# Layers' attentions: VectorE takes the remainder of a split head right behind the step's maximum

## The reference, cut to what matters

```python
h = rms_norm(x, g_mix[layer]);  proj = h @ w_in[layer]
# A: 8 heads of 64; each query sees the 128 keys that an indexer's scores pick (top_k)
p = softmax(where(valid, q_a @ k_a.T * scale, -inf));  out_a = p @ v_a
# B, differential: 4 heads with two query/key pairs of 64 and one value of 128 each
p = softmax(where(admissible, q_b @ k_b.T * scale, -inf))
out_b = rms_norm((p[:, 0] - lam * p[:, 1]) @ v_b, g_subln) * (1.0 - lam_init)
x = x + concatenate([out_a, out_b]) @ w_out[layer]
x = x + (silu(h2 @ w_gate) * (h2 @ w_up)) @ w_down      # h2 = rms_norm(x, g_ffn)
```

## Time and profile before

| | us |
|---|---|
| median of 3 runs | 3299.22 |
| profiled execution, own time | 3299.04 |
| its span | 3297.3 |
| TensorE busy (matmul) | 3135.2 (95%) |
| VectorE busy | 1747.7 (53%) |
| ScalarE busy | 1259.9 (38%) |
| first `Difference` stage | from about 943 to 998 |
| second `Difference` stage | from about 1631 to 1686 |

### The profile page before, as it was taken

How to read it: one execution, slowest core, us unless ns; L and a number is a source line. 1 busy time by engine, 2 the same in 40 slices (tenths; PEclk the granted TensorE clock), 3 DMA queues, 4 the chain that set the end, 5 groups by cost and what they waited for, 6 DMA issues and landing times. The chain is left out here.

```text
span 3297.3 us, 40508 instructions
## 1 busy us (share of the span) xinstructions
PE 3135.2 (95%) x15662; PEld 2623.4 (80%) x15662; DVE 1747.7 (53%) x2591; ACT 1259.9 (38%) x1772; POOL 250.4 (8%) x241
## 2 busy tenths in 40 slices
PE   8979999999989999999899999999899989899998
PEld 6768888788778888888678888787777789688887
DVE  3355666447885443368755343576355454454342
ACT  3335433333474222243653222465344554232222
POOL 0011000003200000004000000001000272000000
PEclk9979999999999999999999999999999999899998
DMA  4211233222113323221133232232324401333221
GB/s 151 90 39 39 90 102 102 77 91 90 41 46 102 100 92 102 80 89 64 42 92 102 89 102 89 78 127 90 115 77 153 140 2 52 136 100 98 93 98 55
DMA packets 181822, 290.21 MB, mean 88 GB/s; under 512 B 12029, under 2 KB 112976, under 8 KB 181161
## 3 DMA queue, kind: packets, MB, share of 16 engines
q1 hardware_dynamic: 181673, 288.18, 26.9%
HBM read 269.13 MB, written 10.60 MB: 85 GB/s over the span
## 5 line engine op out<-in xcount | busy, mean ns | idle before, releaser
L445 DVE TENSOR_TENSOR w_lo<-ring,w_hi 128x2048 fp32r<-128x2048 f32 (+2 forms) x216 | 491.8, 2277 | 611.3 <-ACT w_hi L439 611.1
L272 PE MATMUL psum<-h_hi,w_hi 128*128 128x512 f32 x1824 | 716.9, 393 | 2.4 <-SPq L126 1.5
L274 PE MATMUL psum<-h_hi,w_lo 128*128 128x512 f32 x1824 | 710.0, 389 | 0.0
L273 PE MATMUL psum<-h_lo,w_hi 128*128 128x512 f32 x1824 | 709.9, 389 | 0.0
L439 ACT ACTIVATE w_hi<-ring 128x2048 fp32r<-128x2048 f32 (+2 forms) x216 | 408.1, 1890 | 667.9 <-PE psum L274 657.2
L272 PE MATMUL psum<-s_hi,w_hi 128*128 128x512 f32 x1088 | 430.8, 396 | 25.6 <-DVE s_lo L357 8.8
L274 PE MATMUL psum<-s_hi,w_lo 128*128 128x512 f32 x1088 | 429.6, 395 | 0.0
L273 PE MATMUL psum<-s_lo,w_hi 128*128 128x512 f32 x1088 | 426.8, 392 | 0.0
L272 PEld LDWEIGHTS psum<-h_hi,w_hi 128*128 128x128 f32 x1824 | 342.4, 188 | 82.3 <-issue 10.2
L273 PEld LDWEIGHTS psum<-h_lo,w_hi 128*128 128x128 f32 x1824 | 342.5, 188 | 72.5 <-issue 2.4
L274 PEld LDWEIGHTS psum<-h_hi,w_lo 128*128 128x128 f32 x1824 | 342.4, 188 | 72.0
(11 more groups left out here) (472 smaller groups left out, 3855.8 us busy)
## 6 DMA issues: line engine op xcount, KB each, us to landing
ring<-in_w_in SPq DMA_DIRECT2D x66, 1024.0 KB, 5.1
ring<-in_w_up SPq DMA_DIRECT2D x44, 1024.0 KB, 5.2
ring<-in_w_down SPq DMA_DIRECT2D x33, 1024.0 KB, 4.9
ring<-in_w_gate SPq DMA_DIRECT2D x22, 1024.0 KB, 5.3
ring<-in_w_ffn_in SPq DMA_DIRECT2D x22, 1024.0 KB, 5.1
ring<-in_w_out SPq DMA_DIRECT2D x16, 1024.0 KB, 4.9
ring<-in_w_ffn_down SPq DMA_DIRECT2D x11, 1024.0 KB, 4.8
residual<-sum_rows SPq DMA_DIRECT2D x16, 256.0 KB, 5.8
```

What stands on the lines that cost most here:

```text
L272: nc.tensor.matmul(bank, l_hi, r_hi, start=start, stop=False)
L273: nc.tensor.matmul(bank, l_hi, r_lo, start=False, stop=False)
L274: return nc.tensor.matmul(bank, l_lo, r_hi, start=False, stop=stop)
L445: self.core.nc.vector.tensor_tensor(lo, self.core.raw(s, a)[:, :, 0:n], hi.bitcast(F32), ALU.subtract).then_inc(r.split[s], 1)
```

## The change

The remainder is taken right behind the step's maximum, ahead of the work that goes along. Its condition and its instruction stay as they were.

```diff
                                                    -scale, -PICKED, ALU.add, ALU.min, stats[:, n % 4, :]
                                                    ).then_inc(biased, 1)
+                    if n and split_after(n - 1):
+                        rest(split_after(n - 1))
                     beside.on_vector(dve, n)
                     if first:
                         first.on_vector(dve, n)
-                if n and split_after(n - 1):
-                    rest(split_after(n - 1))
                 if 2 <= n < steps + 2 and by_dve(n - 2):
                     store(dve, n - 2, nc.vector.tensor_copy).then_inc(stored_dve, 1)
```

## The result

The changed kernel takes 3306.23 us as the median of 18 runs, against 3300.15 us of the kernel before in the 18 runs beside it: ratio 1.0019, interval 1.0012 to 1.0026. The forecast was 7.8 us. Ratios are taken over executions at the usual clock, so that two in the experiments, of 3588 and 11802 us at a lower granted clock, are left out, and they need not be the quotient of the two medians. The profiled execution's span is 3308.6 us, 11.3 over before; several microseconds of such a difference are due to the execution and not to the change. In the last experiment, where both kernels ran again unaltered on another chip, the way to the first attention stage differed by up to 5.5 us between the two profiles of one kernel, and the way between the two layers' stages by 3.1.

A forecast was written before the change was run, and what follows sets the result against it. No engine is full; the chain from engine to engine sets the attention stages' pace. Losses of 4.40 and 3.39 us in the two `Difference` stages, together 7.8 on 3299.04, gave 3306.8 us; range 3300 to 3312.

The forecast's parts named there:

- Where the change acts: Emitted order changes only in the two `Difference` stages; in the two `Choose` stages it stays the same, 0 us.
- The chain through a step pair: Steps 10 to 12: remainder, maximum, exponential, Square, rounding, remainder set the pace, 3.07 us; beside-work is no part of it.
- The sum by places: Each place loses the moved work's length less the next remainder's slack: 4.40 us in the first `Difference` stage, 3.39 second.
- Step 24: Last remainder in a `Difference` stage: multiply and w_lo move behind it, loss 1.31 us, least sure, between 0 and 1.31.
- Second stage, step 4: Second `Difference` stage: the remainder comes 0.34 us earlier, so the loss is 0.14 us instead of 0.48.
- Step 6's loss: Second `Difference` stage: the 0.67 us lost is covered at step 8, where TensorE stands 0.69 us for instruction issue.
- rival 1: Faster: remainders come earlier and TensorE's waits for them go, 2 x 2.1 = 4.2 us, to 3294.8; chance 0.08.
- 2 (nothing): Not slower: VectorE catches up in gaps where it waits for scores, late maxima hold up nobody; 3299 us, chance 0.17.
- Rival 3: Slower still: a longer TensorE gap brings a low-clock episode in the tail, 1.4 us a stage; 3310 us, chance 0.25.

## Why the prediction was right

- **Where the change acts**: right. The `Choose` stages didn't change (59.14 us before, 59.11 and 59.12 after).
- **The chain through a step pair**: right, and shown from both ends: the remainder moved ahead meets ScalarE's rounding unfinished (VectorE is idle ahead of it for 0.51 to 1.11 us at steps 4, 6, 8, 10, 18, 20 and 24 of the first stage, and not at all at 14 and 22, where the rounding is done), and what is taken off ScalarE's part of the chain (Square) comes back in full up to step 14.
- **The sum by places**: seven of the eight terms of the first stage are within 0.03 us. Step 24 was 1.31 and is 1.20: the w_lo piece takes 0.70 us when the remainder follows it, and 0.60 ahead of `finish`, as it now stands. The reason that I gave for it, TensorE's wait of 1.32 us, was the wrong one: that wait fell to 0.69 us in one experiment and went in another, and the stage kept its length within 0.2 us. It is VectorE's own row of work behind step 24 that carries the delay. So this term, called the least sure, came out nearly right by a reason that doesn't hold alone.
- **Second stage, step 4**: wrong by 0.3. I took from one trace that its remainder would come 0.34 us earlier. It starts 8.70 us into the stage in both stages of the changed kernel, 8.75 and 8.66 in the two profiles of before. The rounding ended 8.38 us into the stage in the first of these and 8.62 in the second, where the remainder followed it at once: that slack was one execution's, in which the steps behind TensorE's slow start (granted clock 0.50 from 1635.74 to 1637.74 us) came a little sooner, and not the kernel's. Step 6's loss was covered at step 8 (-0.01 in the table), as I put it by the 0.69 us stall of TensorE.
- **Bounds and rivals**: rival 1 (faster) and 2 (nothing) fell, since the remainders came later and nothing was taken up. The argument against rival 1 claimed a little much: at steps 6 and 10 the rounding had ended 0.19 and 0.07 us before the beside-work was through, by the same slacks that the sum uses. Rival 3, the clock, didn't happen in the profiled stages of the changed kernel, but in the same tail, behind the same gap, in a kernel that differs only on ScalarE; its price there is 1.6 us a stage, my estimate was 1.4. The gap itself grew to 2.01 us, not to some 2.6.
- **The size**: 8.0 us by the stages, 7.8 forecast, 6.1 by the medians. The interval of 4.0 to 8.6 us (0.12 to 0.26%) holds all three. That the time itself, 3306.23, is within 0.6 us of the 3306.8 forecast is in part luck: the median of before rose from 3299.22 in 3 runs to 3300.15 in 18, and the smaller difference made up for it. Why both comparisons of medians (1.0019, 1.0018) lie below 1.0024 stays open, though both intervals reach over it; wandering clock episodes of about 3 us are enough to blur it, but no run settles it.

## What to carry to other kernels

VectorE ran its work in the order in which it was emitted: the `scalar_tensor_tensor`, which needed nothing, stood still with the remainder ahead of it and began at 967.84 us, behind the remainder at 967.23. So an instruction that waits should stand behind work that needs nothing. Moving it ahead can help only when what it waits for is already done, and even then what is passed must not be on the chain: at step 24 alone the remainder came 0.56 us earlier and the stage lost 0.65. Before hurrying the operation that TensorE waits for, look at what that operation waits for itself, and whose busy time covers it; here the length of the work moved behind, less the slack of the next wait, gave the cost of seven of the eight places in the first stage to 0.03 us. For a change of this size the length of the stage in two profiles, which repeated to 0.05 us, said more than the medians of ten runs. A slack read from a single trace is worth a second look: the one wrong by 0.3 us was one execution's.

## What the hardware showed that was not expected

- TensorE's granted clock behind the same work, 1.99 us in 4 with a gap of 2.01 in it, was 1.00 in the changed kernel and 0.57 in the one with the rounding ahead, each time in both stages, and 1.6 us of a gain of 2.1 went with it.
- Behind a remainder of a split (64x512, length 0.68) made along with the steps VectorE starts its next operation 0.60 us after the remainder's start for the keys and 0.71 for the queries (967.23 to 967.84, 963.29 to 964.01 in the changed kernel), in all four stages before and after and whatever comes next; among those made ahead of step 0 it is 0.71 for both. No run told why.
